# Gated rows added in DRAM by scatters, and the shared expert among the expert passes

## The reference

```python
def modulate(x, c, w_ada, b_ada):
    shift, scale, gate = jnp.split(c @ w_ada + b_ada, 3, axis=-1)
    h = x * (1.0 + scale[:, None, :]) + shift[:, None, :]
    return h, 1.0 + gate[:, None, :]

def swiglu(x, w1, w3, w2):
    return (jax.nn.silu(x @ w1) * (x @ w3)) @ w2

def moe(h, router_w, router_bias, w1, w3, w2, ws1, ws3, ws2):
    ...
    scores = jax.nn.sigmoid((xt @ router_w).astype(jnp.float32))
    biased = scores + router_bias.astype(jnp.float32)
    ...
    gates = jnp.take_along_axis(scores, eidx, axis=-1)
    gates = gates / jnp.sum(gates, -1, keepdims=True) * ROUTED_SCALE
    ...
    def expert_block(acc, blk):
        tok, wt, e = blk
        y = swiglu(x_pad[tok], w1[e], w3[e], w2[e])
        return acc.at[tok].add(y * wt[:, None].astype(y.dtype)), None
    ...
    out = acc[:T] + swiglu(xt, ws1, ws3, ws2)

def deepnorm_residual(x, y, gate, g, b):
    return layer_norm(ALPHA * x + gate * y, g, b)
```

## Time and profile before

| | us |
|---|---|
| median of three runs (lowest, highest) | 2981.86 (2980.83, 2983.79) |
| the profiled execution, its own time | 2983.08 |
| its span in the trace | 2981.4 |
| attention stage | 58.0 to 836.4 |
| norm stage | 836.4 to 858.7 |
| first expert stage | 858.7 to 1607.1 |
| norm and delta stage | 1607.1 to 2189.0 |
| norm stage | 2189.0 to 2210.8 |
| second expert stage | 2210.8 to 2956.4 |

### The profile page before, as it was taken

One profiled execution on the slowest core, in us unless ns is written; L12 is line 12 of the kernel. 1 busy time (PEld: TensorE's weight loads), 2 busy tenths in 40 slices (PEclk: granted clock), 3 DMA queues, 4 the chain that ended last, 5 costly groups with the idle time before them and its releaser, 6 DMA issues. The chain is left out here.

```text
span 2981.4 us, 31993 instructions
## 1 busy us (share of the span) xinstructions
PE 2661.9 (89%) x11495; PEld 1506.3 (51%) x11496; DVE 1037.0 (35%) x2058; ACT 628.8 (21%) x1263; POOL 360.3 (12%) x396
## 2 busy tenths in 40 slices
PE   6998989899859999999974999999868999999974
PEld 3565556556734444444432476676744444444431
DVE  1434334423361222221138444444352222221138
ACT  0112030311221211221111333433221112111211
POOL 0000001000001111111100122121101111111101
PEclk9999989999969999999986999999978999999987
DMA  6532416243157999999955121221257999999954
GB/s 260 163 109 87 136 49 182 69 127 96 36 224 273 364 382 387 384 378 389 373 228 170 39 83 44 71 70 36 73 197 276 357 386 393 381 385 381 372 236 181
DMA packets 180803, 658.03 MB, mean 221 GB/s; under 512 B 30408, under 2 KB 92200, under 8 KB 125376
## 3 DMA queue, kind: packets, MB, share of 16 engines
q1 hardware_dynamic: 129872, 525.43, 45.9%
q0 software_dynamic: 37632, 104.92, 10.1%
q10 hardware_dynamic: 13168, 25.89, 3.0%
HBM read 624.64 MB, written 60.85 MB: 230 GB/s over the span
## 5 line engine op out<-in xcount | busy, mean ns | idle before, releaser
L1662 PE MATMUL moe_py<-weights_w,moe_hT 128*128 128x512 f32 (+1 forms) x1040 | 375.9, 595 | 3.5 <-ACT moe_hT L1239 3.5
L1648 PE MATMUL moe_ph<-weights_w,moe_xT 128*128 128x512 f32 x832 | 373.4, 602 | 1.8 <-DVE moe_xT L1449 1.8
L1648 PE MATMUL moe_pr<-weights_w,moe_xT 128*64 128x512 f32 (+1 forms) x1248 | 369.7, 596 | 1.1 <-DVE moe_xT L1449 1.1
L862 PE MATMUL attn_proj<-core_hT,attn_w_w 128*128 128x512 f32 x768 | 341.4, 606 | 15.4 <-issue 12.9
L1449 DVE COPY moe_xT<-moe_tx 128x512 f32<-128x512 f32 x104 | 71.9, 691 | 752.1 <-PE moe_tx L1621 752.1
L862 PEld LDWEIGHTS attn_proj<-core_hT,attn_w_w 128*128 128x128 f32 x768 | 149.1, 195 | 201.1 <-issue 197.1
L1648 PEld LDWEIGHTS moe_ph<-weights_w,moe_xT 128*128 128x128 f32 x832 | 155.6, 192 | 179.8 <-issue 179.8
L1648 PEld LDWEIGHTS moe_pr<-weights_w,moe_xT 128*64 128x64 f32 (+1 forms) x1248 | 134.3, 154 | 194.7 <-issue 193.8
L2226 PE MATMUL gdn_pj<-core_hT,gdn_w_w 128*128 128x512 f32 x512 | 226.4, 596 | 0.0
L1290 POOL DMA_INDIRECT y_rows<-moe_ysb,moe_yidx x104 | 105.5, 1015 | 993.1 <-ACT moe_ysb L1248 850.7
L1662 PEld LDWEIGHTS moe_py<-weights_w,moe_hT 128*128 128x128 f32 (+1 forms) x1040 | 140.2, 169 | 163.6 <-issue 156.4
(11 more groups left out here) (366 smaller groups left out, 3018.4 us busy)
## 6 DMA issues: line engine op xcount, KB each, us to landing
weights_w<-in_expert_w_dram SPq DMA_DIRECT2D x384, 1024.0 KB, 12.0
attn_w_w<-in_attn_w_in_dram SPq DMA_DIRECT2D x36, 1024.0 KB, 8.7
weights_w<-y_rows SPq DMA_DIRECT2D x32, 1024.0 KB, 5.3
attn_ada_w<-in_ada_w_dram POOLq DMA_DIRECT2D x64, 384.0 KB, 5.9
gdn_w_w<-in_gdn_w_in_dram SPq DMA_DIRECT2D x16, 1024.0 KB, 6.0
normNone_w<-in_ada_w_dram SPq DMA_DIRECT2D x8, 1536.0 KB, 6.4
attn_swp<-attn_raw ACTq DMA_DIRECT2D x192, 64.0 KB, 2.1
gdn_ada_w<-in_ada_w_dram POOLq DMA_DIRECT2D x32, 384.0 KB, 3.6
```

The lines of the kernel that those rows point to most:

```text
L862: last = nc.tensor.matmul(proj[n % 2][:], w[:, j % SLOTS, kk, half_ * P:(half_ + 1) * P], c.hT[:, kk, :], start=kk == 0, stop=kk == KT - 1)
L1648: last = nc.tensor.matmul(ph[b][at, :], xT[:, b, k, at], w13[:, n % UP, :, k], start=k == 0, stop=k == KT - 1)
L1662: last = nc.tensor.matmul(py[n][at, :], hT2[:, b, k, at], w2[:, load % DOWN, k, half(n)], start=k == 0, stop=k == 1)
```

## The change

**Outputs.** The gate goes with the row number: `num` carries it as three bf16 parts (`COLS` 7 for 5), the same small products bring it to the pass's rows, and VectorE writes `gcol` behind the row number (`to_add`, two steps for one). ScalarE multiplies by it in its output copy. The scatter adds its rows (`compute_op=ALU.add`) to `sums[l]`, which holds two copies of the 512 rows per layer: single passes add to the copy of their place's parity, a pass of two experts adds each to its own copy. POOL waits before a scatter for the last ones on the same copy (`earlier`). SP fills both layers' sums with zeros at the start of the attention stage, 8 copies of 1 MB from DRAM to DRAM.

**Tail.** Four loads of 1 MB, and per tile three steps of VectorE. The steps for further blocks move among the passes 12 to 22.

**Shared expert.** It has weight slots of its own, loaded in the norm stage, and is four items of the sequence without a number p: tiles 0 and 1 while the routing runs, tiles 2 and 3 ahead of the first two double passes. VectorE merges its rows into x (`merge`).

**Norm stage.** TensorE computes the scores there, tile by tile, with `hT` held and 64 columns moving, and SP stores the normalised x, unmodulated, to `x_rows`; the gathered rows are modulated when they are turned (`turn_in`, four steps for one on ScalarE and on VectorE). Constants come from DRAM instead of POOL and VectorE steps. Four experts are fixed ahead of the ranking instead of three (`EARLY`), and the rank with two passes is 4 instead of 3.

```diff
...
-FULL, DOUBLE, PASSES = 38, 3, 52
+EARLY, FULL, DOUBLE, PASSES = 4, 38, 4, 52
+SUMS = 2
+COLS = 7
...
+            weights.load_router(sp)
+            weights.load_shared(sp)
+            weights.load_expert(sp, 0)
+            for t in range(TT):
+                sp.wait_ge(xn_ready, t + 1)
+                sp.dma_start(x_rows[t * P:(t + 1) * P, :], c.x[:, t]).then_inc(weights.x_out, 16)
+            for e in range(1, EARLY):
+                weights.load_expert(sp, e)
...
+            def scores(t):
+                pe.wait_ge(laid_act, t + 1)
+                pe.wait_ge(laid_dve, t + 1)
+                to = logits.rearrange("p k n -> p (k n)")[:, t * NE:(t + 1) * NE]
+                for k in range(KT):
+                    last = nc.tensor.matmul(to, c.hT[:, k, t * P:(t + 1) * P], weights.rw[:, k], start=k == 0, stop=k == KT - 1)
+                if t == TT - 1:
+                    last.then_inc(lg_done, 1)
+
...
+                if weights is not None and t:
...
+                    scores(t - 1)
+            if weights is not None:
+                scores(TT - 1)
...
+            for s in sums:
+                for t in range(TT):
+                    sp.dma_start(s.rearrange("(t p s) d -> t p (s d)", p=P, s=SUMS)[t], zeros_dram.ap()).then_inc(cleared, 16)
...
+        want = EARLY if routed == 0 else 3
+        while n < want and len(ranks) < NE - 2:
+            r = next(ahead, None)
+            if r is None:
+                break
+            at = take(r)
+            seq.append(Pass(routed, [r], [at]))
+            routed, n = routed + 1, n + 1
+            if r == DOUBLE:
+                seq.append(Pass(routed, [r], [at], start=P))
+                routed, n = routed + 1, n + 1
...
+        t = next(tiles, None)
+        if t is not None:
+            seq.append(Pass(None, tile=t))
...
+    def adds_to(i):
+        return range(SUMS) if len(seq[i].ranks) == 2 else [i % 2]
+
+    def earlier(i):
+
+        found = {}
+        for j in range(i):
+            if seq[j].p is not None and set(adds_to(j)) & set(adds_to(i)):
+                found[j % 2] = j
+        return sorted(found.values())
...
-            sp.wait_ge(h_done, last_pass[NE - UP] + 1)
-            for a, name in enumerate(("shared_w1", "shared_w3")):
-                sp.dma_start(ew.up_slot(SHARED_UP, a), A[name][l].rearrange("(p k) n -> p (k n)", k=KT)).then_inc(sh_in, 16)
-            sp.wait_ge(y_done, last_pass[NE - DOWN] + 1)
-            sp.dma_start(ew.down_slot(SHARED_DOWN), A["shared_w2"][l].rearrange("(p k) n -> p (k n)", k=2)).then_inc(sh_in, 16)
-            sp.wait_ge(y_done, PASSES)
+            sp.wait_ge(y_done, ITEMS)
...
-                sp.wait_ge(y_out[b], 16 * (PASSES // 2))
-            for m in range(TT * TOPK // YG):
-                t, k = m * YG // TOPK, m * YG % TOPK
-                if m >= NYG:
-                    sp.wait_ge(yg_used, YG * (m - NYG + 1))
-                sp.dma_start(yg[:, m % NYG], y_rows.rearrange("(t p k) d -> p t k d", p=P, k=TOPK)[:, t, k:k + YG])\
-                  .then_inc(yg_in[m % NYG], 16)
+                sp.wait_ge(y_out[b], all_out[b])
+            for t in range(TT):
+                sp.dma_start(back[:, t], sums[l].rearrange("(t p s) d -> p t s d", p=P, s=SUMS)[:, t]).then_inc(sums_in[t], 16)
...
                 for n in range(2):
-                    nc.scalar.copy(ysb[:, p % 2, half(n)], py[n][:]).then_inc(y_ready, 1)
-            act.wait_ge(y_out[0], 16 * (PASSES // 2))
-            act.wait_ge(y_out[1], 16 * (PASSES // 2))
+                    if ps.p is None:
+                        ins = nc.scalar.copy(ysb[:, i % 2, half(n)], py[n][:])
+                    else:
+                        ins = nc.scalar.activation(ysb[:, i % 2, half(n)], py[n][:], ACT.Copy, scale=gcol[:, ps.p % 4:ps.p % 4 + 1])
+                    ins.then_inc(y_ready, 1)
...
+                                        bounds_check=SUMS * SEQ - 1, oob_is_err=False, compute_op=ALU.add).then_inc(done, 16)
...
+            for i, ps in enumerate(seq):
+                if ps.p is None:
+                    continue
+                if ps.p + 3 < PASSES:
+                    gather_pass(ps.p + 3)
+                pool.wait_ge(y_ready, 2 * i + 2)
+                for j in earlier(i):
+                    pool.wait_ge(y_out[j % 2], scattered(j))
+                scatter(i % 2, ps.p % 4, y_out[i % 2])
...
+            def to_add(s, done):
                 with nc.allow_low_precision(reason="sums of small integers"):
-                    return nc.vector.tensor_reduce(yidx[:, s:s + 1], pi[:, 2:5], AX.X, ALU.add)
+                    nc.vector.tensor_reduce(sidx[:, s:s + 1], pi[:, 2:4], AX.X, ALU.add).then_inc(done, 1)
+                nc.vector.tensor_reduce(gcol[:, s:s + 1], pi[:, 4:COLS], AX.X, ALU.add).then_inc(done, 1)
+
+            def turn_in(b):
+                for k in range(4, KT):
+                    last = nc.vector.tensor_scalar(xT[:, b, k], tx[1][:, k - 4], by[:, k:k + 1], plus[:, k:k + 1], ALU.mult, ALU.add)
+                return last
...
+            def merge(i):
+                y, t = ysb[:, i % 2], seq[i].tile
+                dve.wait_ge(y_ready, 2 * i + 2)
+                ch.do(nc.vector.scalar_tensor_tensor(out=y, in0=c.ada[:, 2], scalar=1.0, in1=y, op0=ALU.add, op1=ALU.mult))
+                ch.sync()
+                nc.vector.scalar_tensor_tensor(out=c.x[:, t], in0=c.x[:, t], scalar=ALPHA, in1=y, op0=ALU.mult, op1=ALU.add)\
+                    .then_inc(merged, 1)
...
-                if p + 3 < PASSES:
+                if i + 1 < ITEMS:
+                    product(i + 1)
+                if p is not None and p + 3 < PASSES:
                     if p >= 1:
-                        dve.wait_ge(y_out[(p + 3) % 2], 16 * ((p - 1) // 2 + 1))
-                    to_write((p + 3) % 4).then_inc(idx_ready, 1)
+                        before_p = seq.index(routed[p - 1])
+                        dve.wait_ge(y_out[before_p % 2], scattered(before_p))
+                    to_add((p + 3) % 4, idx_ready)
...
             for t in range(TT):
-                a = acc[:, t % 2]
-                for k in range(TOPK):
-                    n, m = t * TOPK + k, (t * TOPK + k) // YG
-                    dve.wait_ge(yg_in[m % NYG], 16 * (m // NYG + 1))
-                    src, scale = yg[:, m % NYG, k % YG], gate[:, t, k:k + 1]
-                    if k == 0:
-                        nc.vector.tensor_scalar(a, src, scale, None, ALU.mult).then_inc(yg_used, 1)
-                    else:
-                        nc.vector.scalar_tensor_tensor(out=a, in0=src, scalar=scale, in1=a, op0=ALU.mult, op1=ALU.add).then_inc(yg_used, 1)
-                    dve.wait_ge(yg_used, n + 1)
-                dve.wait_ge(sh_y, t + 1)
-                for n in range(2):
-                    nc.vector.tensor_tensor(a[:, half(n)], a[:, half(n)], py[n][:], ALU.add).then_inc(sh_acc, 1)
-                dve.wait_ge(sh_acc, 2 * t + 2)
-                ch.do(nc.vector.scalar_tensor_tensor(out=a, in0=c.ada[:, 2], scalar=1.0, in1=a, op0=ALU.add, op1=ALU.mult))
+                s = back[:, t, 0]
+                dve.wait_ge(sums_in[t], 16)
+                ch.do(nc.vector.tensor_tensor(s, s, back[:, t, 1], ALU.add))
                 ch.sync()
-                ch.do(nc.vector.scalar_tensor_tensor(out=c.x[:, t], in0=c.x[:, t], scalar=ALPHA, in1=a, op0=ALU.mult, op1=ALU.add))
+                ch.do(nc.vector.scalar_tensor_tensor(out=s, in0=c.ada[:, 2], scalar=1.0, in1=s, op0=ALU.add, op1=ALU.mult))
+                ch.sync()
+                ch.do(nc.vector.tensor_tensor(c.x[:, t], c.x[:, t], s, ALU.add))
...
+            up_of(1, range(KT // 4, KT))
+            turn_h_of(0)
+            pe.wait_ge(num_ready, 1)
+            rows_of(0)
+            down_of(0)
+            rows_of(1)
+            turn_h_of(1)
+            rows_of(2)
             turn_x_of(0)
-            pe.wait_ge(idx_ready, 6)
-            up_of(0)
+            down_of(1)
+            up_of(2)
             turn_x_of(1)
...
```

More of the change, by code:

```diff
@@ L468, in _ @@
             rows = [(c.ada[:, 0], vector(A["ln_g"])), (c.ada[:, 1], vector(A["ln_b"])), (c.ada[:, 2], part(2))]
-            if weights is not None:
-                rows = [(weights.rows[:, 1], part(1)), (weights.rows[:, 0], part(0))] + rows
             for to, v in rows:
@@ new lines, in __init__ @@
+        table = np.concatenate([np.eye(P), np.ones((P, P)), own < np.arange(P), num.reshape(P, -1),
+                                np.broadcast_to(offs.reshape(-1), (P, SUMS * COLS))], 1)
+        self.constb_dram = nc.inline_tensor(np.ascontiguousarray(table.astype(mybir.dt.np(BF16))), f"expert_constbs{l}")
+        self.constb = st.sb("constb", list(table.shape), BF16)
+        self.identb, self.onesb, self.before = (self.constb[:, n * P:(n + 1) * P] for n in range(3))
+        at = 3 * P + TT * COLS * NE
@@ new lines, in _ @@
+            silu(0)
+            act.wait_ge(gate_turned, 1)
```

(27 more changed lines are left out.)

688 lines of the change are left out of this document (315 added, 373 removed).

## The result

The changed kernel takes **3030.18 us** (median of 4 runs, 3026.51 to 3034.22) against 2982.82 us beside it: 1.0156 times as long, 95% interval 1.0136 to 1.0176. The likeliest case, 2949 us, was wrong in sign; the rival that came nearest, 3039, had a chance of 0.25. The profiled execution took 3028.7 us with a span of 3026.8, 45.4 more than before.

The account below looks back on a forecast made before the run. TensorE's work (busy 89% of the span) plus the places where it has none was taken as the bound. Two stages of (-56 + 21 + 3 + 15) = -17, and +1, gave -33: 2981.9 to 2949 us, range 2912 to 3050.

Parts of the forecast that it names:

- The tail: End of each expert stage: 32 VectorE multiply-adds go, further-block steps move among the passes; 56 us less, bounds 50 to 58.
- The shared expert in the sequence: Expert passes: two of four shared passes stand in the sequence at 10.6 us each, fully on TensorE's path; +21 a stage.
- The start: Norm stage to first expert matmul: norm stage 7 us longer, expert stage's start 3.6 shorter; net +3, bounds -2 and +9.
- POOL's order of adds: Scatters wait on POOL for the last one on their copy; claimed to cost nothing while a landing stays under one pass.
- "+15 a stage": Scatters in the passes: 0.84 us more per pass for reading target rows; singles just free, 13 double passes about 1.1 each.
- 9.5 us: Expert passes: a scatter landing up to this long is free; each us beyond costs a us per pass.
- Rival 2: Expert passes: DMA engines become the bound, +43 a stage, 32 after weights' slack; 2983 us, no change; chance 0.17.
- the slack of weights: Expert passes: weight landings may grow from 7.1 to 20 us without a wait, absorbing some 11 a stage.
- a DMA share of 0.98 or above: Profile after, expert passes: with waits of L1689 or L1716 on weights, this would show that the DMA engines bind.
- rival 3: Expert passes: read-modify-write lengthens landings, TensorE waits at L1661 in every pass; +60 a stage, 3039 us; chance 0.25.
- the 1.2 that the prediction names: Scatter landings: 1.2 us more than 9.5 on average over all passes was said to eat the whole gain.
- The zeros: Start of attention: 22 us of DMA copies, covered by 30.30 us of TensorE projections; +1 once, bounds 0 and 10.

## Why the prediction was wrong

**Right.** The tail: -56 forecast, -55.1 and -54.9 measured, with three steps a tile as worked out. The shared expert in the sequence: +21 forecast, 21 to 24 measured. The start: +3 forecast, within -2 to +9, and -1.3 and -1.2 measured; the norm stage grew by 9 instead of 7, and the expert stage's start fell to 31.6 us where I had 38, since the routing ended inside the two shared up projections and the first gather, issued 23 us into the stage, landed unnoticed under the shared downs. POOL's order of adds held nothing back that counts: 9.1 us in one wait between 1200 and 1500.

**Wrong: "+15 a stage" for the scatters.** The time per pass was right: 0.84 us forecast, 0.91 measured. The step that failed is where they were put. I added them to the landing of one scatter, asked whether it still fitted into 9.5 us, and let it cost only what stuck out. But 0.84 us of *all* DMA engines is no delay of one transfer. It is demand, and the earlier trace rows had said that 0.96 is taken. Divided by a share that has no room to grow, it lengthens every pass of the stretch, whatever waits first. Rival 2 said just this and had the size, 43 a stage; measured are 48 and 44. It then took 11 off for the slack of weights, which the runs don't show, and got a chance of 0.17 only, although its row for saturation was the plainest in the profile. Its own sign was wrong too: it looked for a DMA share of 0.98 or above, and the share stayed between 0.93 and 0.97 from 1100 to 1500. The sign that came was the lower rate at the same share. The Trainium skill ("Collectives: The Full Stack", the bandwidth ceiling) puts the halved rate of a ReduceScatter down to a second source read per add, not to the add. The trace agrees with its factor of two: 327 ns for an adding packet of 4 KB against 159 for a plain one. That the extra 168 ns are the read of the target row is not shown by any record here, since the bytes are counted the same with and without adds.

**Right in sign and nearly in time, for another reason: rival 3.** It had 3039 us, by landings past 9.5 us. These came (10.6) and TensorE did wait for them, but with that wait gone the time stayed. So to be near was luck. Its price was also not consistent with the sum: by 32 us of gain a stage over 52 passes, 0.6 us more a pass eats the gain, not the 1.2 that the prediction names. A wait that the profile names can be the place where a shortage shows and not the shortage.

**Wrong: the zeros, +1.** 14.8 measured, over the bound of 10. I named the tables behind the zeros as a risk and set its bound by a guess. The step that failed is the cover: 30 us of projections on TensorE were to hide the zeros, but 16.7 us into them TensorE stood for 13.0 us, waiting through ScalarE and VectorE for a table. The zeros' own 22 us at 384 GB/s are near what the table took to land, 21.8, and behind it come 8 us of table steps before TensorE can go on.

Together: -33 forecast. In both stages the passes cost 142.5 for 72 (+70.5), the start is 8.5 better, the tail 2 worse, the zeros 13.8 worse, other stages +0.8. That gives +46, and the spans differ by 45.4.

## What to carry to other kernels

When a resource is at its ceiling, price each new use as so much time of that resource, not as latency that may hide behind something. The test is one division: bytes moved by busy share; if the rate per busy share falls (here 384 / 0.96 = 400 before, 350 / 0.94 = 372 after), the work has become dearer, and here no rearrangement of waits brought it back. Before adding rows in DRAM to shorten a tail, look whether the stretch that issues the adds has idle DMA time, and whether something cheaper stands in the tail: here some wide VectorE steps, moved among the passes, were worth 38 us in the whole kernel.

## What the runs showed of the hardware

- A packet of one 4 KB row takes a DMA engine 327 ns in an adding scatter and 159 ns in a plain one (medians over the whole of after, and of before and the run without adds).
- An adding indirect scatter of up to 128 rows of 4 KB lands in 6.1 us with no other load (the last of the stage), where the plain one took 3.2; in the saturated stretch 10.6 for 8.7. GpSimd is busy 1.58 us with each instead of 1.0, and this time is part of both landings. The line of the scatters in after (duration in ns, min/median/max):

```profile
L1371 POOL DMA_INDIRECT sums<-moe_ysb,moe_sidx x23: 1582/1583/2057, 1208.8 to 1498.1; - x23
```

- With a quarter of the down weights the DMA engines were at 0.85 between 1200 and 1300, and a row number step could still come 11.5 us after the start of its scatter while a pass of two experts ran. That the weights of two experts at once do it is my reading; no run tried it.
- Behind many of TensorE's waits of some 2 us the granted clock falls to half for 3.4 us (in some cases 6.8), and the same up projection then takes 8.8 us for 7.13. Not behind each: in the run with fewer weight bytes after eight of nine, in after not behind waits of 2.29 and 1.89 us. The stretch 1400 to 1500 has 0.95 on average, and 1.00 without the waits. Of the 48 us that the adds cost in the first stage, 15 are this.
- Small tables issued among 8 MB of DRAM-to-DRAM copies, on another queue, landed after 21.8 us instead of 3.6, and after 31.0 in another run.
